# A float32 transformer kernel on one core: the perceptrons' products read tokens and write sums in another order

## What is computed

```python
def squared_relu_mlp(h, w1, w2):      # w1: 1024 x 4096, w2: 4096 x 1024
    a = jax.nn.relu(h @ w1)
    return (a * a) @ w2
...
    h = rmsnorm_2(x, norm_gains[layer, 1])
    x = x + squared_relu_mlp(h, mlp_w1[layer], mlp_w2[layer])
```

## Time and profile before

| | |
|---|---|
| median of 3 runs | 1901.47 us |
| the profiled execution | 1902.51 us |
| its span, first to last instruction | 1900.7 us |
| TensorE (PE) busy | 1861.3 us, 98% |
| GpSimd (POOL) busy | 1088.4 us, 57% |
| VectorE (DVE) busy | 1049.9 us, 55% |
| ScalarE (ACT) busy | 853.3 us, 45% |
| mean granted TensorE clock | 0.995 of 2.4 GHz |

### The profile page before, as it was taken

How to read it: one execution, slowest core, us unless ns; L and a number is a source line. 1 busy time by engine, 2 the same in 40 slices (tenths; PEclk the granted TensorE clock), 3 DMA queues, 4 the chain that set the end, 5 groups by cost and what they waited for, 6 DMA issues and landing times.

```text
span 1900.7 us, 28284 instructions
## 1 busy us (share of the span) xinstructions
PE 1861.3 (98%) x10454; PEld 1572.3 (83%) x10454; DVE 1049.9 (55%) x1863; ACT 853.3 (45%) x1562; POOL 1088.4 (57%) x1321
## 2 busy tenths in 40 slices
PE   8999999999999999999999999999999999999998
PEld 6888777888888878877888899878888888999887
DVE  5648664522223377776765555475755476555552
ACT  4555454542333356565534344344434354444341
POOL 5428333445556433425788888644433278888882
PEclk9999999999999999999999999999999999999999
DMA  6214222233333312112233333332222133333331
GB/s 191 59 34 123 56 56 57 61 84 97 91 102 113 87 56 68 56 46 78 89 100 103 98 100 101 100 96 82 67 67 57 45 100 100 102 99 90 101 111 56
DMA packets 269162, 160.42 MB, mean 84 GB/s; under 512 B 6137, under 2 KB 267489, under 8 KB 268898
## 3 DMA queue, kind: packets, MB, share of 16 engines
q1 hardware_dynamic: 269026, 158.61, 29.1%
HBM read 156.50 MB, written 2.10 MB: 83 GB/s over the span
## 4 chain that ended last, share of the span: by engine, by line
PE 84%; DVE 5%; POOL 5%; ACT 4%; issue 2%; DMA 0%; ACTq 0%; DVEq 0%; SPq 0%
PE bank L259 18%; PE bank L2004 9%; PE bank L622 7%; PE bank L624 7%; PE bank L623 7%; POOL weight_lo L241 3%; PE bank L2649 3%; PE bank L2651 3%; PE bank L2650 3%; PE bank L1602 3%; PE bank L1604 2%; PE bank L1603 2%; PE bank L424 2%; PE bank L425 2%; PE bank L426 2%
## 5 line engine op out<-in xcount | busy, mean ns | idle before, releaser
L241 POOL TENSOR_TENSOR weight_lo<-weight_stage,weight_hi 128x256 fp32r<-128x256 f32 x1160 | 964.8, 865 | 731.3 <-ACT weight_hi L229 731.3
L229 ACT ACTIVATE weight_hi<-weight_stage 128x1024 fp32r<-128x1024 f32 (+2 forms) x303 | 309.2, 1022 | 251.9 <-PE bank L259 180.0
L259 PE MATMUL bank<-hidden_hi,weight_lo 128*128 128x512 f32 x512 | 200.6, 392 | 4.9 <-POOL weight_lo L241 4.9
L622 PE MATMUL bank<-a_hi,weight_lo 128*128 128x512 f32 (+1 forms) x464 | 198.3, 427 | 2.0 <-POOL weight_lo L241 1.2
L259 PE MATMUL bank<-hidden_lo,weight_hi 128*128 128x512 f32 x512 | 199.4, 390 | 0.0
L259 PE MATMUL bank<-hidden_hi,weight_hi 128*128 128x512 f32 x512 | 199.4, 389 | 0.0
L624 PE MATMUL bank<-a_hi,weight_hi 128*128 128x512 f32 (+1 forms) x464 | 182.8, 394 | 0.0
L623 PE MATMUL bank<-a_lo_rounded,weight_hi 128*128 128x512 f32 (+1 forms) x464 | 182.7, 394 | 0.0
L1980 POOL TENSOR_TENSOR block_weight_lo<-block_weight,block_weight_hi 128x256 fp32r<-128x256 f32 x156 | 124.7, 826 | 52.6 <-ACT block_weight_hi L2139 52.6
L2354 DVE TENSOR_TENSOR x_t<-x_t,bank 128x512 f32<-128x512 f32 x128 | 82.0, 678 | 90.3 <-PE bank L259 90.3
L259 PEld LDWEIGHTS bank<-hidden_hi,weight_lo 128*128 128x128 f32 x512 | 96.1, 188 | 26.0 <-issue 6.9
(11 more groups left out here) (393 smaller groups left out, 4371.2 us busy)
## 6 DMA issues: line engine op xcount, KB each, us to landing
weight_stage<-in_mlp_w SPq DMA_DIRECT2D x128, 512.0 KB, 3.7
weight_stage<-in_w_in SPq DMA_DIRECT2D x57, 512.0 KB, 3.7
weight_stage<-in_hg_w_in SPq DMA_DIRECT2D x32, 512.0 KB, 3.9
weight_stage<-in_sb_w_qkv SPq DMA_DIRECT2D x24, 512.0 KB, 3.6
weight_stage<-in_w_mkv SPq DMA_DIRECT2D x8, 512.0 KB, 3.8
weight_stage<-in_w_out SPq DMA_DIRECT2D x8, 512.0 KB, 3.9
weight_stage<-in_sb_w_o SPq DMA_DIRECT2D x8, 512.0 KB, 3.8
weight_stage<-in_hg_w_o SPq DMA_DIRECT2D x8, 512.0 KB, 3.8
```

What stands on the lines that cost most here:

```text
L229: act.activation(self.hi[slot][:, 0:size], self.stage[slot][:, 0:size], ACT.Copy).then_inc(self.hi_done, 1)
L241: last = pool.tensor_tensor(self.lo[slot][:, part], self.stage[slot][:, part], self.hi[slot][:, part].bitcast(F32), ALU.subtract)
L259: last = pe.matmul(out, l, r, start=n == 0, stop=n == 3 * len(pairs) - 1)
L622: pe.matmul(to, wlo, ahi(k), start=k == 0, stop=False)
```

## The change

`products` (all its uses: L259) and `block` (L2004) hand the same moving tile and the same part of the same PSUM bank to each matmul, but as a three-dimensional pattern. The 512 tokens are seen as 4 pieces of 128, each of 8 lines of 16 elements (64 bytes). The matmul takes line 0 of all four pieces, then line 1 of all four, and so on; the sums are written in the same order, so each sum ends where it was before. With 256 tokens there are 2 pieces. No instruction, wait or tile is added or taken away, and the weight loads are as before.

```diff
@@ -248,6 +248,14 @@
+LINE = 16
+
+
+def by_lines(ap, n):
+
+    return ap.rearrange("p (i j e) -> p j i e", i=n // P, j=P // LINE, e=LINE)
+
+
 def products(pe, out, pairs, before=None):
...
         for l, r in ((wlo, ahi), (whi, alo), (whi, ahi)):
-            last = pe.matmul(out, l, r, start=n == 0, stop=n == 3 * len(pairs) - 1)
+            last = pe.matmul(by_lines(out, T), l, by_lines(r, T), start=n == 0, stop=n == 3 * len(pairs) - 1)
             n += 1
@@ -2001,7 +2009,8 @@
                     for l, r in ((wl, ah), (wh, al), (wh, ah)):
-                        last = pe.matmul(to, l, r, start=begins and i == 0, stop=i == 11, skip_group_check=True)
+                        last = pe.matmul(by_lines(to, HALF), l, by_lines(r, HALF), start=begins and i == 0, stop=i == 11,
+                                         skip_group_check=True)
                         i += 1
```

## The result

The kernel after takes 1909.44 us, the median of 5 runs (1909.09 to 1909.74), beside 1901.47 us before. The ratio is 1.0045, with a 95% interval of 1.0034 to 1.0056: slower by 8 us. The forecast was 1884 us; its range, 1866 to 1945 us, holds the time, by the part that came from a rival whose mechanism turned out not to be at work.

What follows compares the result with a forecast made beforehand. TensorE was taken to bound the kernel. Gains of 11.7 us (512 tokens) and 5.6 us (256 tokens) sum to 17.3 us; 1902.5 - 17.3 - 1.0 = 1884 us, range 1866 to 1945 us.

Steps and rivals of the forecast that it cites:

- What bounds the kernel: Both stretches with L259 and L2004: TensorE bounds them, busy 683.3 of 691 us, so each nanosecond per matmul counts.
- What a matmul costs now: L259: 226.6 ns a turn, against 216.0 ns free-running, so 10.6 ns of each are stalls.
- meetings of the moving stream with the weight load: L259 and L2004: both streams conflict according to their places within 512 bytes; one better address relation is worth 6.4 ns.
- The read order for 512 tokens: L259: one meeting left per matmul, 1824 x 6.4 ns = 11.7 us gained; bounds 19.3 us gain, 13 us loss.
- The read order for 256 tokens: L2004: streams walk nearly in step and may never meet; 5.6 us gained, half of 11.2 us.
- The address pattern itself: L259 and L2004: 32 or 16 runs of 64 bytes per matmul cost nothing, reading or writing.
- The rest: Bank eviction waits as before; GpSimd, with 67 and 78 us to spare in the two stretches, stays hidden behind TensorE.
- a run has a price: L259 and L2004: each of 93,300 64-byte runs costs up to one clock tick, 38.9 us, 1940 us; chance 0.20.
- In step and in conflict: L2004: streams at one pace meet on all eight lines, 80 us lost, 1970 us in all; chance 0.13.
- Nothing changes: L259 and L2004: the stall is a fixed piece at each float32r matmul's start; 1898 to 1905 us; chance 0.15.

Runs made afterwards that it cites:

- the sixteen: A program of float32r matmuls alone, moving tile at four places 64 bytes apart against weights at four; 512 columns took 227.5 ns at equal places, otherwise 229.6 to 233.3 ns.
- The program: Float32r matmuls alone, no other engine at work, 24 of each arrangement of places and read orders; 256 columns by lines took 120.0 ns at all eight weight places.

## Why the prediction was wrong

*What bounds the kernel* was right in the main: of the 10.5 us that the two lines were busy longer, 8.4 us came through in the two stretches, and no engine took over. The middle stretch, with the matmuls that the change leaves alone, kept its length (305.4 and 305.3 us).

*What a matmul costs now* was right in its size. The floor of 216.0 ns is what bfloat16 shows (215.7 ns). The Trainium skill gives N/2.4 GHz + about 2.5 ns for back-to-back matmuls of N columns (TensorE: Matmul & The Clock Gate, section "Wait — 56ns, not 53.3ns?"), 215.7 ns for 512; bfloat16 agrees, float32r at 226.7 ns doesn't. It was wrong in what the 10.6 ns are. The prediction took them from L2004, whose pairings differ by 6.4 ns, for meetings of the moving stream with the weight load. With 32 columns of weights the stall is larger (232 ns a turn), and it grows along the stream. The weights take part all the same: their place within 256 bytes moves a contiguous turn between 226.7 and 233.3 ns, and the best of these lies below the turn with a short load.

*The read order for 512 tokens* is the step that failed. It took 6.4 ns less a matmul, 11.7 us in all, from one meeting with the weight load less; instead 4.9 ns more came in the settled turn, 7.5 us in all (421.28 to 428.75 us busy). Equal places were not a meeting to be avoided. L259 had them, and no placement of the sixteen is better: beside a load of 128 columns the contiguous read is 5 ns faster than beside one of 32, while the read by lines takes 231 to 234 ns beside either. By these turns most of what the change costs is that advantage given up; a longer stall of the stream itself is the smaller part (0 ns with 32 columns of weights in one program, 2 ns in the other). The period is 256 bytes, not 512, so "64 bytes of every 512" keeps the stream at one of four places for four lines. How the order sets the turn is known as a table only: four lines at a place 232 ns, eight 239, all 242, but two lines 240, and backwards, with a new place for every line, 234. The bound on the side of loss, 7 ns, held; but no chance was given to it, since the slower cases were the two rivals alone.

*The read order for 256 tokens:* the aligned 1560 kept 120.0 ns where 117 or less was expected. The three pairings did draw together, but upward: the two favourable ones lost 6.4 and 2.7 ns. L2004 took 3.0 us more, where 5.6 us less were forecast. The program shows the same 120.0 ns by lines wherever the weights lie.

*The address pattern itself* was right on the writing side, at nothing. On the reading side it leaned on the durations of records of 128 columns, not on turns; at the full rate the order of the reads is all of the loss. *The rest* was right.

The rivals: *a run has a price* ended on the right side but is not what happened. It wanted L259 to grow by twice what L2004 grows, and the aligned L2004 grew by nothing; equal numbers of runs cost 7 and 20 us, and the writes cost nothing. *In step and in conflict* fell with the aligned 120.0 ns. *Nothing changes* fell with the 4.9 ns. The case that came, a favourable relation of the two streams lost by the new order, was in no rival. Two rows spoke against the meetings it was built on: L259 at equal places was stalled by as many ns as L2004, in spite of twice the columns, so no count of meetings per column fitted both.

Why a float32r stream stalls itself, why a full weight load at an equal place shortens its turn, and by what rule a pair of streams settles into one pattern or another, stays open. The split between the stream's own stall and the load was measured in the programs alone, with the weights at an equal place, and never with no load at all. The runs show the table, not the circuit.

## What to carry over

Before reordering a stream to dodge a conflict, show that the other party is in it: shrink the other stream, and see both whether the stall goes and whether the difference between the two orders goes. Here the stall stayed and the difference went. Measure the period of an address effect with a program of 24 matmuls a placement before building on it. A placement that is good for one group of matmuls depends on the group that ran ahead of it, so look at its neighbours' turns after moving a tile.

## What the runs showed of the hardware

- A float32r matmul of 512 columns at 2.4 GHz takes 226.7 ns in the best arrangement tried, and 215.7 in bfloat16. With 128 columns of weights, equal places of both operands within 256 bytes are best for 512 columns (227 against 230 to 233 ns), and not for 256 columns (120.0 against 113 to 118 ns).
- Beside a weight load of 128 columns at an equal place, the order of a 4-byte read costs by the places within 256 bytes: pieces of 256 bytes nothing (226.5 ns), 64 of every 512 bytes 5 ns, 64 of every 256 bytes 12 to 13 ns, one place 15 ns, runs of 16 bytes 40 ns. Beside a load of 32 columns 64 of every 512 bytes cost 0 to 2 ns. Writing PSUM in runs of 64 bytes costs nothing, and bfloat16 reads by lines cost nothing.
- The same placement can hold two lasting patterns, 113.4 and 117.7 ns, and which one holds depends on what ran before.
